# Sliding-window attention between dense fillers: a new order of ScalarE's and VectorE's work in each step

## The reference, cut to what matters

```python
def sliding_window_attention(q, k, v, sinks):
    ...
    scores = jnp.einsum('bnqhgd,bnkhd->bnhgqk', qb, kb) * scale      # 128 queries x 256 keys
    scores = jnp.where(valid[None, :, None, None], scores, NEG_INF)
    m = jnp.maximum(jnp.max(scores, axis=-1, keepdims=True), sink)
    p = jnp.exp(scores - m)
    p = p / (jnp.sum(p, axis=-1, keepdims=True) + jnp.exp(sink - m))
    out = jnp.einsum('bnhgqk,bnkhd->bnqhgd', p.astype(v.dtype), vb)
```

## Time and profile before

| | us |
|---|---|
| median of three runs (lowest, highest) | 2418.4 (2416.87, 2419.04) |
| the profiled execution, its own time | 2417.04 |
| span of its trace | 2415.3 |
| PE busy in the span | 2361.2 (98%) |
| DVE busy | 1526.2 (63%) |
| ACT busy | 979.7 (41%) |
| granted TensorE clock | 0.999 of full speed |

### The profile page before, as it was taken

One profiled execution on the slowest core, in us unless ns is written; L12 is line 12 of the kernel. 1 busy time (PEld: TensorE's weight loads), 2 busy tenths in 40 slices (PEclk: granted clock), 3 DMA queues, 4 the chain that ended last, 5 costly groups with the idle time before them and its releaser, 6 DMA issues.

```text
span 2415.3 us, 30564 instructions
## 1 busy us (share of the span) xinstructions
PE 2361.2 (98%) x11300; PEld 1957.8 (81%) x11300; DVE 1526.2 (63%) x2395; ACT 979.7 (41%) x1675; POOL 139.7 (6%) x189
## 2 busy tenths in 40 slices
PE   8999898999999999999999999999999999999998
PEld 6787777778888888888788888898888888888886
DVE  6746767656777764434654663374499888883335
ACT  6335555533344342223043243264354444442124
POOL 1000000011000010112000020012100000000000
PEclk9999999999999999999999999999999999999999
DMA  5112223235323243331111033263122222244313
GB/s 198 41 44 71 70 70 114 71 113 133 103 88 96 88 164 98 103 115 49 53 44 31 27 109 92 85 197 125 37 68 85 89 87 78 78 140 139 104 61 123
DMA packets 253361, 222.19 MB, mean 92 GB/s; under 512 B 7246, under 2 KB 225571, under 8 KB 252226
## 3 DMA queue, kind: packets, MB, share of 16 engines
q1 hardware_dynamic: 233920, 148.39, 20.2%
q0 software_dynamic: 15424, 56.53, 7.4%
q10 hardware_dynamic: 3906, 15.78, 2.0%
HBM read 171.39 MB, written 49.28 MB: 91 GB/s over the span
## 4 chain that ended last, share of the span: by engine, by line
PE 80%; DVE 11%; ACT 5%; issue 2%; DMA 1%; SPq 0%; ACTq 0%; DVEq 0%
PE bank L993 10%; PE bank L994 10%; PE bank L995 10%; PE bank L1589 4%; PE bank L1590 4%; PE bank L1591 4%; PE bank L1226 4%; PE bank L1228 4%; PE bank L1227 4%; DVE Sx L2820 2%; PE bank L1630 2%; PE bank L1632 2%; PE bank L1631 2%; ACT Sx L1878 2%; ACT q_hi_twice L1871 2%
## 5 line engine op out<-in xcount | busy, mean ns | idle before, releaser
L1705 ACT ACTIVATE whi<-wraw 128x1024 fp32r<-128x1024 f32 (+2 forms) x159 | 160.5, 1009 | 481.3 <-PE bank L995 263.6
L2624 DVE TENSOR_TENSOR wlo<-wraw,whi 128x1024 fp32r<-128x1024 f32 (+1 forms) x174 | 204.4, 1175 | 143.5 <-ACT whi L1705 137.5
L1176 PE MATMUL bank<-xhi,whi 128*128 128x512 f32 x384 | 149.6, 390 | 0.0
L1178 PE MATMUL bank<-xhi,wlo 128*128 128x512 f32 x384 | 149.6, 390 | 0.0
L1177 PE MATMUL bank<-xlo,whi 128*128 128x512 f32 x384 | 149.6, 390 | 0.0
L1878 ACT ACTIVATE Sx<-Sx,small 128x256 f32<-128x256 f32 x128 | 63.6, 498 | 158.8 <-DVE small L2826 158.8
L993 PE MATMUL bank<-x2hi,whi 128*128 128x512 f32 x240 | 93.9, 391 | 0.0
L994 PE MATMUL bank<-x2lo,whi 128*128 128x512 f32 x240 | 93.4, 389 | 0.0
L995 PE MATMUL bank<-x2hi,wlo 128*128 128x512 f32 x240 | 93.4, 389 | 0.0
L1630 PE MATMUL bank<-ffn_hi,whi 128*128 128x512 f32 x240 | 93.4, 389 | 0.0
L1631 PE MATMUL bank<-ffn_lo,whi 128*128 128x512 f32 x240 | 93.4, 389 | 0.0
(11 more groups left out here) (529 smaller groups left out, 6620.3 us busy)
## 6 DMA issues: line engine op xcount, KB each, us to landing
wraw<-in_w_in_dram SPq DMA_DIRECT2D x85, 512.0 KB, 3.9
wraw<-in_ffn_w_up_dram SPq DMA_DIRECT2D x44, 512.0 KB, 3.8
filler_spill<-filler POOLq DMA_DIRECT2D x24, 512.0 KB, 3.2
ffn_spill<-ffn_value SPq DMA_DIRECT2D x22, 512.0 KB, 3.4
gate<-filler_spill POOLq DMA_DIRECT2D x16, 512.0 KB, 3.9
wraw<-in_xattn_wkv_dram SPq DMA_DIRECT2D x16, 512.0 KB, 3.9
wraw<-in_ffn_w_down_dram SPq DMA_DIRECT2D x16, 512.0 KB, 3.7
ffn_raw<-ffn_spill ACTq DMA_DIRECT2D x14, 512.0 KB, 4.6
```

The lines of the kernel that those rows point to most:

```text
L1176: pe.matmul(ps(m % 3), whi[slot][:, k, :], xh, start=(k == 0), stop=False)
L1178: last = pe.matmul(ps(m % 3), wlo[slot][:, k, :], xh, start=False, stop=(k == KT - 1))
L1705: act.activation(whi[slot][:, 0:n, 0:m], wraw[slot][:, 0:n, 0:m], ACT.Copy).then_inc(s_whi, 1)
L2624: dve.tensor_tensor(wlo[slot][:, 0:n, :], wraw[slot][:, 0:n, :], whi[slot][:, 0:n, :].bitcast(F32), ALU.subtract).then_inc(s_wlo, 1)
```

## The change

The change moves calls within the two loops over u, on ACT and on DVE. PE, POOL and SP have the same rows as before; each engine issues the same instructions, in another order.

```diff
@@ ScalarE
             for u in range(UNITS):
                 if u == 0:
                     split(T_F + 1, (T_F + 1) % 2)
-                splits_due(u, False)
                 unit_hi(u)
+                if u >= 2:
+                    turned_hi(u - 2)
+                if u >= 1:
+                    exps(u - 1, (u - 1) % 2)
                 if u == 0:
                     q_sum(1)
-                if u >= 2:
-                    turned_hi(u - 2)
+                if u == 1:
+                    query_root(1)
                 if u >= 3:
                     keep_o(u - 3)
+                splits_due(u, False)
                 splits_due(u, True)
-                exps(u, u % 2)
-                if u == 1:
-                    query_root(1)
             t = T_F + FILL_IN
+            turned_hi(UNITS - 2)
+            exps(UNITS - 1, (UNITS - 1) % 2)
             splits_due(UNITS, False)
-            turned_hi(UNITS - 2)
             keep_o(UNITS - 3)
@@ VectorE
             for u in range(UNITS):
                 if u == 0:
                     split(T_F + 1, (T_F + 1) % 2)
-                splits_due(u, False)
+                if u >= 1:
+                    load_rq(u - 1)
+                    maxima(u - 1)
+                if u == 2:
+                    query_inverse(1)
+                if u >= 2:
+                    turned_lo(u - 2)
                 unit_lo(u)
                 if u >= 1:
+                    halves_due(u - 1, False)
                     normalise(u - 1, (u - 1) % 2)
-                if u >= 2:
-                    turned_lo(u - 2)
+                if u == 1:
+                    query_var(1)
                 if u >= 3:
                     sum_o(u - 3)
-                if u == 1:
-                    query_var(1)
+                splits_due(u, False)
                 halves_due(u, True)
                 splits_due(u, True)
-                load_rq(u)
-                maxima(u)
-                halves_due(u, False)
-                if u == 1:
-                    query_inverse(1)
             t = T_F + FILL_IN
+            load_rq(UNITS - 1)
+            maxima(UNITS - 1)
+            halves_due(UNITS - 1, False)
+            turned_lo(UNITS - 2)
+            normalise(UNITS - 1, (UNITS - 1) % 2)
             splits_due(UNITS, False)
-            normalise(UNITS - 1, (UNITS - 1) % 2)
-            turned_lo(UNITS - 2)
             sum_o(UNITS - 3)
```

## The result

The changed kernel took 2376.14 us (median of four, 2374.57 to 2377.73) against 2418.69 (2416.87 to 2419.04) in runs of both on one chip: 42.6 us less, ratio 0.9825, 95% interval 0.9813 to 0.9837. The forecast was 2378.4, in 2375 to 2390.

What follows compares the result with a forecast made beforehand. PE was taken to wait for a serial ring through ACT and DVE, no engine being full. 36.6 us from 29 units and 3.45 from the first, 40.0 in all, gave 2378.4 us, range 2375 to 2390.

Steps and rivals of the forecast that it cites:

- a ring: PE waits at its transposes for a serial ring of maxima, exponentials, query parts, scalings, low parts; 1.26 us a unit.
- The walk through one iteration: An iteration timed from its turn: ACT and DVE finish before PE asks, so a unit costs 9.62 us.
- a full iteration: An iteration with a split and two halves, two in eight; the next maxima start at 10.05 us, nothing carries over.
- the three margins (scores, turn, split): Spare time before PE asks: scores 3.6 us, the next turn 2.3, the split's `wlo` 3.6.
- The term of 29 units: Turn 1 to turn 30: each unit falls from 10.88 to 9.62 us, 36.6 us gained.
- The first unit: Turn 0 to turn 1: 12.06 us falls to 8.61, 3.45 us gained, bounds 0 and 3.45.
- Behind the stage: After 508.60 us PE has no waits and releases all its partners, so the 40.0 us gain is kept whole.
- The wait column: Gain summed from PE's profiled waits: 31.0 us and some 3 in the first unit, 34 us and 2384.
- the starts: Gain read from start times of PE's instructions instead of its waits: 40.0 us, giving 2378.4.
- (a): Wait moves from the turn to the scores; `qlo` 4.9 us later than worked takes the whole gain, 2418; chance 0.03.
- (b): The ring remains in part: 3 us more makes a unit 10.4 us, 2402; lighter forms 2381 to 2392; chance 0.08.
- (c): Slower: exponentials behind a `pthi` waiting for PE stretch the ring past 10.88 us; 4.0 us extra gives 2434; chance 0.03.

Runs made afterwards that it cites:

- run 5: Kernel before with one more ScalarE copy between the wait for the maxima and the exponentials of every unit: 2444.01 us, ratio 1.0106.
- run 6: Changed kernel with one more ScalarE copy between the wait for the maxima and the exponentials: 2376.64 us, ratio 0.9830.
- run 7: Kernel before with 8 filler steps a unit in place of 10, the same work in all: 2447.70 us, ratio 1.0119.
- run 8: Changed kernel with 8 filler steps a unit in place of 10, the same work in all: 2376.14 us, ratio 0.9826.
- run 1: Only ScalarE has the new order, VectorE has that of the kernel before: 2400.23 us, ratio 0.9926.
- run 3: Changed kernel with the transposed low parts back behind the scalings on VectorE: 2376.28 us, ratio 0.9825.
- run 4: Changed kernel with the late splits back at the head of the iteration on both engines: 2375.83 us, ratio 0.9826.
- run 10: Changed kernel with both the low parts back behind the scalings and the late splits back at the head: 2376.57 us, ratio 0.9830.
- run 11: The changed kernel once more, unedited, for a second trace: 2375.60 us, ratio 0.9829.
- run 2: Only VectorE has the new order, ScalarE has that of the kernel before: 2479.55 us, ratio 1.0254.
- run 9: Changed kernel with 6 filler steps a unit, 12 tiles inside the units and 12 behind: 2402.12 us, ratio 0.9939.

## Why the prediction was right, point by point

**What bounds the kernel now**: a ring, not an engine. Shown by runs 5 and 6, and by 7 and 8: ACT's load and PE's load were each changed alone, and each time the order decided whether it mattered.

**The walk through one iteration** held within 0.4 us at every station, in a full iteration too, and the three margins (scores, turn, split) were all kept. What of the moves carries the gain was not asked in the prediction; runs 1, 3, 4 and 10 together point to ScalarE's exponentials behind the query part and `pthi`, with a late split that VectorE does not have to wait for. Low parts in front and splits at the end are not needed for it, and VectorE's half alone does harm.

**The term of 29 units** was 36.6 us and measured 315.55 - 276.66 = 38.9. The term that was mis-sized is PE's own work, 9.62 us by the prediction and 9.54 in the trace. Its pieces were read at a turn that had waited, where the first instructions are a little further apart: turn to weigh 0.82 against 0.79 now, last score to turn 0.16 (read at turn 0, which came just as its release did) against 0.12, weigh to filler 1.01 against 1.00. 0.08 us by 29 is the 2.3.

**The first unit** was to give 3.45 us, with turn 1 near 189.6; it stands at 189.35. From turn 0 to turn 1 it took 8.64 us, against 8.61 worked out and 12.06 before. Turn 0 itself came earlier, at 180.71 against 180.99, which the prediction did not have. It is no part of the mechanism: run 3, which is the same program up to there, has it at 181.12.

**Behind the stage** the gain is kept whole: the span of the second trace is 2415.3 - 2372.7 = 42.6 us shorter, and its turns 0, 1 and 30 (180.61, 189.25, 465.90) give 0.4 + 3.4 + 38.9 = 42.7. The first trace is 40.9 shorter, by the 1.7 us of run 11.

**The wait column** gave 34 us and 2384, the starts 40 and 2378.4; the runs are at 2376.1. The column has 33.4 us in all (the 34 counted the wait at turn 1 twice), while the starts show 38.9 in the 29 units alone. The reason stands in the two windows: for the same work of these units PE counts as busy 284.86 us with the waits and 276.66 without, 8.2 more; with the 30.7 idle that is 38.9. A score has a length of 0.28 us and the next starts 0.12 later, and only the last one before a wait is counted in full. The Trainium skill, Perfetto Trace Analysis, section Tensor Engine Instruction, calls a matmul's end in the profile an estimate; the trace agrees by these 8.2 us.

**The rivals** (a), (b) and (c) did not occur in the changed kernel. Run 2 waits at the scores as in (a) and is slower than before as in (c), though by another link: there `pthi` stands behind the exponentials, not the other way round. Run 9 waits for the scalings as in (b), with VectorE nearly full as well.

## What to carry to other kernels

Where engines hand work round, walk one iteration from the durations in the trace and ask for each hand-over how long before the demand it ends; the engine that is named as the releaser may be only the last link, and moving it alone may do nothing. Where one engine waits for the other's long piece and then for its short one, taking up the short pieces first shortens the ring: here the query part and `pthi` ahead of the exponentials. Write down the order of each loop as a circle before you call a move a shift, since a call written into the next iteration can stand in its old place. One engine's half of a change can be worse than none, as VectorE's was here. Two cheap tests tell a ring from a full engine: add a fixed piece of idle work to a stage, and take cover away from the engine that waits.

## What the runs showed of the hardware

The granted clock of PE fell in some of the slower kernels, which was not expected. It was 0.999 over the span before in the profiled execution (0.996 to 0.999 over all of that kernel's, 0.997 to 0.999 over those of the changed one), and 0.988 in run 2, 0.993 in runs 5 and 7. In run 5 a window (length, PE busy, ..., clock) shows where:

```profile
255.00:260.00 5.00, 4.64 (x15) 4.07 (x16) 4.26 (x15) 1.24 (x4) 0.37 (x1) 0.50 0.01 2
```

and its timeline of PE what came before and after:

```profile
252.55 0.39 PE L1142 MATMUL bank<-k_stacked,q_hi_twice 128*128 128x256 f32 x1 [0.95 <-DVE qlo L2799]
...
255.36 1.94 PE L1153 MATMUL bank<-ident,Sx 128*128 128x128 f32 x8 [1.60 <-DVE ptlo L2848]
...
258.81 0.63 PE L1177 MATMUL bank<-xhi,whi 128*128 128x512 f32 x1
259.23 0.63 PE L1178 MATMUL bank<-xlo,whi 128*128 128x512 f32 x1
```

After a wait of 0.95 us, eight short matmuls and a wait of 1.60 us the fillers start 0.42 us apart instead of 0.23: that is the level of 1.2 GHz instead of 2.4. Such waits do not always bring it: the kernel before waited up to 1.6 us at 25 of its turns, and 1.45 and 1.47 us close behind each other before 190.36 and 193.05 us, and kept the full clock in that trace.

What it costs depends on what PE has in hand. In run 1 the unit from turn 1 to turn 2 had no late split and PE was never idle in it:

```profile
192.61:203.67 11.06, 11.06 (x50) 9.50 (x51) 7.33 (x23) 6.01 (x14) 0.00 (x0) 0.86 0.00 1
```

Behind waits of 0.65 and 1.48 us it took 11.06 us in place of 9.54, and another one, from 389.74 us on, 11.20 at a clock of 0.85: 3.2 us of that run are the clock. Where PE waits for the ring anyway it costs little. In run 5 the units grew by 0.76 us and the copy is 0.72, so the clock adds 1 us or so over the 29. Of the 5 us of run 5 that lie outside them, 2.8 lie before turn 0, 0.5 in the first unit, and 1.6 in the unit behind turn 30, which took 14.36 us in place of 12.74, with a clock of 0.88 from 533 to 547 us; for the first 2.8 the cause stays open beyond the copy itself. In run 7 a unit has 2.20 us of waits, as expected without any clock, and in run 2 PE is not on the chain. So the losses of runs 2, 5 and 7 are in the main the longer rings, and a wait on PE can cost more than its length where PE itself sets the pace behind it.
